# State updates of the samples as 32-row products from two row groups

## The chip, the cores and the metric

The kernel runs on the 8 cores of one Trainium2 chip. Each core takes one prompt of the batch of 8 and 16 of the 128 samples, and no core talks to another. The time is that of one execution on the device, in microseconds, of the slowest core. The median of three runs of the kernel before is 1225.57 us (1224.73 to 1225.89). Arrays are laid out and permuted on the host ahead of the launch and behind it; that is not part of the time.

## What is computed

Two layers, each with gated linear attention (4 heads, keys of 128, values of 256), a pooling branch and a merge of the two. The prompt has 16 meta tokens and 2048 tokens of its own. What matters here is the attention state of the samples. Each of a core's 16 samples brings 4 new tokens, and per layer and head a state S of 128 x 256 in float32. From the reference, for one sample and head, with b the cumulative log-forget over the 4 tokens:

```
o     = (intra-token part) + (q * exp(b)) @ S
kd    = k * exp(b_last - b)                       # 4 x 128
S_new = exp(b_last)[:, None] * S + kd.T @ v       # 128 x 256
```

All 16 x 4 x 2 = 128 states of a core are read, used for o, updated and written.

## The kernel before

*Tiling.* A core's tokens are 17 tiles: tile 0 holds the samples' 64 rows (sample s in rows 4s to 4s+3) and the 16 meta rows, 80 rows in all; 16 tiles of 128 prompt tokens follow. They are grouped in five chunks. Per layer and head, `att_unit` (L909) does the attention of a chunk: projections for k, q, v and the gate, scores, state recurrence, norm. For chunk 0 it also leaves the samples' operands: `kd0` (L473), the decayed keys of 80 rows by 128, `v0` (L471), the values of 80 rows by 256, and `q0`, the queries as 128 by 64.

*A batch of samples.* `sample_batch(l, h, j)` (L1064) updates the states of four samples of one head; j runs from 0 to 3, so there are 2 x 4 x 4 = 32 batches. Its work is emitted in three steps, parted by `yield`. First, GpSimd multiplies `kd0` with four columns of a row mask (`rowm`, a constant that is 1 in the four rows of one sample) into `kdm`: for each sample a copy of the 80 x 128 keys with all rows of other samples zero. A DMA on SyncE's queue brings the four states, ScalarE casts them to bf16, TensorE makes eight products of 4 columns for o, and VectorE copies these into `osT`. In the second and the third step, TensorE makes two products each, of all 80 rows of a masked key copy and of `v0`; both go to the two halves of one bank of PSUM, and VectorE then updates the two states in place by `scalar_tensor_tensor`. The third step ends with the DMA that writes the states. `sample_out` (L1097) later turns `osT` with float32 products into 64 partitions and adds it to the intra-token part.

*Banks.* Eight banks, in two groups of four that are handed out in turn (`bank`, L530): "P" for projections, "G" for all else, the sample products too.

*Order.* `weave` (L1149) alternates the steps of `att_unit` with those of `sample_batch` and others, which sets the order in which instructions are emitted. `list_schedule` (L145) then simulates the five engines with a cost for each instruction and fixes each engine's order: among the instructions that are ready, the one emitted first. A product's cost there is max(columns, 128) / 2.4 + 3 ns, whatever its rows. At run time each engine takes its instructions in that order and waits on semaphores.

*Helpers.* All products are issued at L551 and the transposes at L556, so the profile shows these lines; `tt` is L579, `stt` L591, `cp` L598 (L570 on ScalarE), `dma` L611. In the profile `kdm`, `osT` and the states are parts of `sb_Y`, `kd0` and `v0` of `sb_ar`, `q0` of `sb_zq`, `rowm` of `sb_invcnt`, and the decay factors are `sb_ebcm`.

Of the kernel before, what the change touches and what calls it, by code (L numbers as in the profile page):

```python
# [10 lines left out]
ALU = mybir.AluOpType  # L11
# [4 lines left out]
NCORE = 8  # L16
NSS = 16
TS = 4
NS = NSS * TS
NMETA = 16  # L20
NM = NS + NMETA
# [27 lines left out]
WP_C = WP_H + 4 * 6144  # L49
WP_O = WP_C + 8 * 3584  # L50
WP_TOT = WP_O + 8192

CF_IDENT = 0
CF_CAUS = 128
# [2 lines left out]
CF_ROWMASK = CF_INVCNT + 64  # L57
# [285 lines left out]
def make_consts():  # L343
    cf = np.zeros((128, NCF), np.float32)
    cf[:, CF_IDENT:CF_IDENT + 128] = np.eye(128, dtype=np.float32)
    j = np.arange(128)[:, None]
    i = np.arange(128)[None, :]
    cf[:, CF_CAUS:CF_CAUS + 128] = (j <= i).astype(np.float32)
    for a in range(NM):
        for b in range(NM):  # L350
            if a < NS and b < NS:
                ok = (a // TS == b // TS) and a <= b
            else:
                ok = a >= NS and b >= NS and a <= b
            cf[a, CF_MASKM + b] = 1.0 if ok else 0.0
    inv = np.zeros((4, NMETA), np.float32)
    for g, w in enumerate(WIN):
        for p in range(NMETA):
            inv[g, p] = 1.0 / min(w, p + 1)
    cf[:, CF_INVCNT:CF_INVCNT + 64] = inv.reshape(1, -1)  # L360
    for a in range(NM):
        cf[a, CF_ROWMASK + (a // TS if a < NS else NSS)] = 1.0
    for blk, m in ((0, 0), (1, 1), (2, 0), (3, 1), (4, 2), (6, 0)):
        cf[16 * blk:16 * blk + 16, CF_SPLIT + m] = 1.0
    return cf


def build_nc():
    nc = bass.Bass("TRN2", target_bir_lowering=False)

    def din(name, shape, dt=F32):
        return nc.dram_tensor(name, list(shape), dt, kind="ExternalInput").ap()

    def dout(name, shape, dt=F32):
        return nc.dram_tensor(name, list(shape), dt, kind="ExternalOutput").ap()
# [4 lines left out]
    sgla = din("sgla", [NL, NSS, 4, 128, 256])  # L380
    spool = din("spool", [NL, NSS, 15, 512])
    wpk = din("wpk", [NL, 128, WP_TOT])
    wal8 = din("wal8", [NL, 128, 512])
# [8 lines left out]
    nsg_s = dout("nsg_s", [NL, NSS, 4, 128, 256])  # L392
# [6 lines left out]
    with contextlib.ExitStack() as st:  # L399
# [48 lines left out]
        rowm = invcnt[:, 64:81]  # L448
# [18 lines left out]
        S_bfs, S_bfs_k = Y.take(1024, BF16)  # L467
        kdm, kdm_k = Y.take(2048, BF16)
        osT, osT_k = Y.take(128)
        ar1b = ar1[:, :].bitcast(BF16)  # L470
        v0, v0_k = ar1b[:, 0:256], ["v0"]  # L471
        on0, on0_k = ar1b[:, 256:512], ["on0"]
        kd0, kd0_k = ar1b[:, 512:640], ["kd0"]  # L473
# [3 lines left out]
        q0, q0_k = zq0[:, 2 * NM:2 * NM + NS // 2].bitcast(BF16), ["q0"]  # L477
# [33 lines left out]
        for i in range(2):  # L511
            a = X.take(512, at=2048 + i * 4096)
            b = X.take(512, at=2048 + i * 4096 + 2048)
            mrg.append((a, b))
        a = X.take(512, at=0)
# [14 lines left out]
        def bank(p):  # L530
            ids = pools[p]
            i = ids[bpos[p] % len(ids)]
            bpos[p] += 1
            S.bank_gen[i] = S.bank_gen.get(i, 0) + 1
            return banks[i], "B%d@%d" % (i, S.bank_gen[i])
# [4 lines left out]
        def fsz(ap):  # L540
            n_ = 1
            for d_ in list(ap.shape)[1:]:
                n_ *= int(d_)
            return n_

        def mm(out, lhsT, rhs, start, stop, r, w, sgc=False):
            N = fsz(rhs)
            c = max(N, 128 if N > 8 else 64) / 2.4 + 3.0
            if lhsT.dtype == F32:
                c *= 4.0  # L550
            return S.add("pe", lambda e: e.matmul(out, lhsT=lhsT, rhs=rhs, start=start, stop=stop,  # L551
                                                  skip_group_check=sgc), r=r, w=w, cost=c, lat=300.0, attach=True)
# [5 lines left out]
        def act(out, in_, func, r, w, bias=None, scale=None, accum_out=None):  # L558
            kw = {}
            if bias is not None:  # L560
                kw["bias"] = bias
            if scale is not None:
                kw["scale"] = scale
            if accum_out is not None:
                kw["accum_out"] = accum_out
            c = 180.0 + 0.83 * fsz(in_) + (210.0 if accum_out is not None else 0.0)
            if not isinstance(bias, (int, float, type(None))) or not isinstance(scale, (int, float, type(None))):
                c += 90.0
            tset = 1 if func == AF.Ln else (0 if func in (AF.Exp, AF.Tanh) else None)
            return S.add("act", lambda e: e.activation(out=out, in_=in_, func=func, **kw), r=r, w=w, cost=c, lat=150.0,  # L570
                         tset=tset)

        def ecost(eng, n_, f=1.0):
            if eng == "pool":
                return 250.0 + 1.7 * n_ * f
            return 130.0 + 1.06 * n_ * f

        def tt(eng, out, in0, in1, op, r, w, cost=None):
            return S.add(eng, lambda e: e.tensor_tensor(out=out, in0=in0, in1=in1, op=op), r=r, w=w,  # L579
                         cost=cost or ecost(eng, fsz(out)), lat=150.0)  # L580
# [9 lines left out]
        def stt(out, in0, scalar, in1, op0, op1, r, w):  # L590
            return S.add("dve", lambda e: e.scalar_tensor_tensor(out=out, in0=in0, scalar=scalar, in1=in1, op0=op0,  # L591
                                                                 op1=op1), r=r, w=w, cost=ecost("dve", fsz(out)),
                         lat=150.0)

        def cp(eng, out, in_, r, w):
            if eng == "act":
                return act(out, in_, AF.Copy, r, w)
            return S.add(eng, lambda e: e.tensor_copy(out=out, in_=in_), r=r, w=w,  # L598
                         cost=ecost(eng, fsz(out), 0.7 if eng == "dve" else 1.0), lat=150.0)
# [14 lines left out]
        def V(ap2d, nchunk, n):  # L614
            return ap2d[:, 0:nchunk * n].rearrange("p (c m) -> p c m", m=n)
# [448 lines left out]
        def sample_batch(l, h, j):  # L1064
            i = cnt["sin"] % 2
            cnt["sin"] += 1
            s_ap, sk = S_in[i]
            hp = h % 2
            em, emk = ebcm[:, 17 * hp:17 * hp + 17], "ebcm%d" % hp
            km = kdm[0:NM, 512 * j:512 * j + 512]  # L1070
            kmk = kdm_k[4 * j:4 * j + 4]
            tt("pool", V(km, 4, 128), kd0[0:NM, :].unsqueeze(1).to_broadcast([NM, 4, 128]),
               rowm[0:NM, 4 * j:4 * j + 4].unsqueeze(2).to_broadcast([NM, 4, 128]), ALU.mult, r=kd0_k + ["inv"], w=kmk)
            dma(V(s_ap, 4, 256), sgla[l, 4 * j:4 * j + 4, h].rearrange("s d v -> d s v"), r=[], w=sk)
            cp("act", S_bfs, s_ap, r=sk, w=S_bfs_k)
            bo, bok = bank("G")
            for sl in range(4):
                for d in range(2):
                    mm(bo[:, d * 16 + sl * 4:d * 16 + sl * 4 + 4], S_bfs[:, sl * 256 + d * 128:sl * 256 + (d + 1) * 128],
                       q0[:, (4 * j + sl) * 4:(4 * j + sl) * 4 + 4], True, True, r=S_bfs_k + q0_k, w=[bok])  # L1080
            cp("dve", V(osT, 2, 64)[:, :, 16 * j:16 * j + 16], V(bo, 2, 16), r=[bok], w=osT_k)
            for s2 in range(2):
                yield
                bp, bpk = bank("G")
                for jj in range(2):
                    s = 4 * j + 2 * s2 + jj
                    mm(bp[:, jj * 256:(jj + 1) * 256], kdm[0:NM, s * 128:(s + 1) * 128], v0[0:NM, :], True, True,
                       r=kmk + v0_k, w=[bpk])
                for jj in range(2):
                    s = 4 * j + 2 * s2 + jj  # L1090
                    o = (2 * s2 + jj) * 256
                    kx = sk[4 * (2 * s2 + jj):4 * (2 * s2 + jj) + 4]
                    stt(s_ap[:, o:o + 256], s_ap[:, o:o + 256], em[:, s:s + 1], bp[:, jj * 256:(jj + 1) * 256],
                        ALU.mult, ALU.add, r=kx + [emk, bpk], w=kx)
            dma(nsg_s[l, 4 * j:4 * j + 4, h].rearrange("s d v -> d s v"), V(s_ap, 4, 256), r=sk, w=[])

        def sample_out(l, h):  # L1097
# [97 lines left out]
        for l in range(NL):  # L1195
# [9 lines left out]
            def s_(*js):  # L1205
                return [(sample_batch(l, 0, j), 2.0) for j in js]
# [86 lines left out]
def _pack_weights(w_in, w_a, pool_w, w_b, w_out):  # L1293
    wp = np.zeros((NL, 128, WP_TOT), np.float32)

# [61 lines left out]
```

How the kernel before makes its waits and increments, by code:

```python
            def run_engine(ename, eng):  # L294
                seen = {}
                for op in ops:
                    if op["eng"] != ename:
                        continue
                    need = {}
                    for d in op["kept"]:
                        sk, val = ops[d]["token"]
                        if need.get(sk, 0) < val:
                            need[sk] = val
                    items = [(sk, val) for sk, val in need.items() if seen.get(sk, 0) < val]
                    attach = items.pop() if (items and op.get("attach")) else None
                    for sk, val in items:
                        eng.wait_ge(sems[sk], val)
                        seen[sk] = val
                    inst = op["fn"](eng)
                    if attach is not None:
                        inst._wait_ge(sems[attach[0]], attach[1])
                        seen[attach[0]] = attach[1]
                    if op["token"] is not None:
                        sk, val = op["token"]
                        inst.then_inc(sems[sk], 16 if op["dma"] else 1)
                if ename == "sp":
                    for k, v in self.dma_final.items():
                        sk = ("dma",) + k
                        if seen.get(sk, 0) < v:
                            eng.wait_ge(sems[sk], v)
```

## Time and profile before

| | before |
|---|---|
| median of three runs | 1225.57 us |
| the profiled execution | 1224.85 us |
| its span, slowest core (all: 1221.9 to 1223.1) | 1223.1 us |
| TensorE busy | 1151.9 us |
| VectorE / ScalarE / GpSimd busy | 676.9 / 573.5 / 467.0 us |
| granted TensorE clock, mean of the span | 0.988 |

One execution is profiled on every core; the rows are those of the slowest, core 1. The span is from its first to its last instruction. PE is TensorE's products, PEld its weight loads, DVE is VectorE, ACT ScalarE, POOL GpSimd, SP SyncE. Busy time is the union of the instructions' durations, and a product's duration reaches to its end, while the next one may start before that. A form such as 80\*128 80x256 is a weight of 80 rows and 128 columns and 80 rows of 256 columns that stream through it.

### The profile page before, as it was taken

The page shows a single profiled execution, that of the slowest core. Times are in us where ns is not written, and L with a number is a line of the kernel's source. Part 1 is how long each engine was busy: PE and PEld are TensorE (multiplying, and loading weights), DVE is VectorE, ACT ScalarE, POOL GpSimd, SP SyncE. Part 2 cuts the span into 40 slices and gives each one's busy share as a digit, 9 for nine tenths or more (in the row PEclk, how much of TensorE's full clock was granted, in tenths as well). Part 3 has the DMA queues.
Part 4 walks back from the last instruction along what each step waited for, and adds up shares of the span by engine and source line. Part 5 has one row for each costly group of instructions (what it writes and reads, how often), then busy time and mean ns, then how long its engine had stood idle before and what let it go on. Part 6 is the DMA issues. An engine that isn't in the chain of part 4 may idle for free.

```text
span 1223.1 us, 22742 instructions; the slowest of 8 cores (1221.9 to 1223.1 us)
## 1 busy us (share of the span) xinstructions
PE 1151.9 (94%) x7616; PEld 691.5 (57%) x7616; DVE 676.9 (55%) x1255; ACT 573.5 (47%) x1279; POOL 467.0 (38%) x754
## 2 busy tenths in 40 slices
PE   1579899999999999999999999999999999999997
PEld 1245457767676555555545555676777555555543
DVE  4466877766765222226776776666667422223555
ACT  2777665666564222222653744665665422222222
POOL 2467755333323222221136686344242222222221
PEclk9789999999999999999999999999999999999999
DMA  9461047362429123114465514725243923211544
GB/s 200 90 155 40 19 76 159 101 136 76 105 87 175 31 39 58 18 30 157 139 158 140 105 47 87 144 71 121 86 89 93 186 33 59 35 19 26 178 166 155
DMA packets 68591, 118.90 MB, mean 97 GB/s; under 512 B 4188, under 2 KB 46556, under 8 KB 68442
## 3 DMA queue, kind: packets, MB, share of 16 engines
q1 hardware_dynamic: 48570, 81.46, 20.9%
q0 software_dynamic: 19904, 35.98, 20.1%
q8 instruction: 60, 0.98, 0.3%
q14 instruction: 57, 0.47, 0.1%
HBM read 117.89 MB, written 36.24 MB: 126 GB/s over the span
## 4 chain that ended last, share of the span: by engine, by line
PE 85%; DVE 4%; ACT 3%; issue 3%; POOL 2%; DMA 1%; SPq 0%; DVEq 0%; POOLq 0%; ACTq 0%
PE bank L551 83%; PE bank L556 3%; DMA sb_OT<-wal 1%; POOL sb_OT L579 1%; ACT sb_Y L570 1%; DVE sb_X L598 1%; DVE sb_X L591 1%; ACT L570 1%; ACT sb_OT L570 1%; DVE sb_Y L585 0%; DVE sb_ast L579 0%; DVE sb_XN L579 0%; DVE sb_MB L811 0%; DVE sb_Y L591 0%; POOL sb_rst L579 0%
## 5 line engine op out<-in xcount | busy, mean ns | idle before, releaser
L551 PE MATMUL bank<-sb_XN,sb_RG 128*128 128x384 bf16 (+2 forms) x3280 | 664.4, 346 | 10.8 <-DVE sb_XN L579 4.4
L551 PEld LDWEIGHTS bank<-sb_XN,sb_RG 128*128 128x128 bf16 x3280 | 316.3, 98 | 248.1 <-issue 8.2
L591 DVE SCALAR_TENSOR_TENSOR sb_X<-sb_X,bank 128x384 f32<-128x384 f32 (+2 forms) x240 | 140.7, 594 | 255.1 <-PE bank L551 234.0
L570 ACT ACTIVATE sb_X<-bank,sb_halfc 128x384 f32<-128x384 f32 (+2 forms) x160 | 97.9, 615 | 250.0 <-PE bank L551 214.4
L570 ACT ACTIVATE sb_X<-bank 128x256 bf16<-128x256 f32 (+6 forms) x328 | 145.9, 464 | 96.2 <-PE bank L551 80.7
L579 POOL TENSOR_TENSOR sb_MB<-sb_X 128x384 bf16<-128x384 f32 (+2 forms) x80 | 88.0, 1100 | 203.7 <-DVE sb_X L591 203.3
L551 PE MATMUL bank<-sb_OT,sb_RG 128*128 128x384 bf16 (+2 forms) x680 | 143.6, 344 | 5.5 <-DVE sb_OT L591 4.2
L551 PE MATMUL bank<-sb_RG,sb_XN 128*128 128x256 bf16 (+1 forms) x1088 | 145.5, 272 | 1.1 <-ACT sb_OT L570 1.1
L570 ACT ACTIVATE sb_Y<-sb_Y 128x1024 bf16<-128x1024 f32 (+1 forms) x79 | 83.5, 1057 | 120.9 <-DVE sb_Y L591 101.6
L551 PE MATMUL bank<-sb_RG,sb_MB 128*128 128x512 bf16 (+1 forms) x544 | 125.3, 379 | 0.0
L579 POOL TENSOR_TENSOR sb_OT<-sb_OT 128x398 f32<-128x398 f32 (+12 forms) x122 | 112.5, 922 | 30.1 <-ACT sb_OT L570 14.0
L551 PEld LDWEIGHTS bank<-sb_RG,sb_XN 128*128 128x128 bf16 (+1 forms) x1088 | 104.5, 99 | 18.0 <-ACT sb_OT L570 1.4
L551 PEld LDWEIGHTS bank<-sb_OT,sb_RG 128*128 128x128 bf16 x680 | 66.5, 98 | 63.1 <-DVE sb_OT L591 7.3
L551 PE MATMUL bank<-sb_X 128*128 128x256 bf16 (+2 forms) x520 | 87.7, 259 | 2.4 <-DVE sb_X L598 2.2
L551 PEld LDWEIGHTS bank<-sb_RG,sb_MB 128*128 128x128 bf16 (+1 forms) x544 | 53.5, 99 | 57.9
L611 POOL DMA_DIRECT2D sb_RG<-wpk x60 | 45.9, 765 | 104.7 <-PE bank L551 74.2
L591 DVE SCALAR_TENSOR_TENSOR sb_OT<-bank,sb_halfc,sb_X 128x384 bf16<-128x384 bf16 (+1 forms) x80 | 47.8, 638 | 63.1 <-PE bank L556 63.1
L579 POOL TENSOR_TENSOR sb_X<-sb_X,sb_ebc 128x384 bf16<-128x384 bf16 (+1 forms) x40 | 35.1, 877 | 117.7 <-DVE sb_X L598 111.3
L551 PE MATMUL bank<-sb_YP,sb_RG 128*128 128x384 bf16 (+2 forms) x320 | 70.8, 343 | 0.0
L570 ACT ACTIVATE sb_OT<-bank 128x384 f32<-128x384 f32 (+6 forms) x120 | 48.3, 438 | 42.8 <-PE bank L551 28.2
L591 DVE SCALAR_TENSOR_TENSOR sb_X<-sb_X,sb_ebc,bank 128x256 f32<-128x256 f32 x128 | 60.5, 473 | 13.1 <-PE bank L551 12.9
L587 POOL TENSOR_SCALAR sb_rst<-sb_rst 128x1 f32<-128x1 f32 (+1 forms) x51 | 11.9, 233 | 139.9 <-ACT sb_Y L570 138.8
(94 smaller groups left out, 1202.8 us busy)
## 6 DMA issues: line engine op xcount, KB each, us to landing
sb_RG<-wpk POOLq DMA_DIRECT2D x40, 512.0 KB, 8.3
sb_Y<-sgla SPq DMA_DIRECT2D x32, 512.0 KB, 4.3
nsg_s<-sb_Y SPq DMA_DIRECT2D x32, 512.0 KB, 2.8
sb_Y<-xp SPq DMA_DIRECT2D x28, 512.0 KB, 5.1
sb_RG<-wpk POOLq DMA_DIRECT2D x16, 896.0 KB, 10.8
H<-sb_Y SPq DMA_DIRECT2D x16, 512.0 KB, 3.6
sb_Y<-H SPq DMA_DIRECT2D x16, 512.0 KB, 3.8
y_p<-sb_Y SPq DMA_DIRECT2D x16, 512.0 KB, 2.6
```

The lines of the kernel that those rows point to most:

```text
L551: return S.add("pe", lambda e: e.matmul(out, lhsT=lhsT, rhs=rhs, start=start, stop=stop, skip_group_check=sgc), r=r, w=w, cost=c, lat=300. ...
L556: return S.add("pe", lambda e: e.transpose(out, in_, ident), r=r, w=w, cost=c, lat=300.0, attach=True)
L570: return S.add("act", lambda e: e.activation(out=out, in_=in_, func=func, **kw), r=r, w=w, cost=c, lat=150.0, tset=tset)
L579: return S.add(eng, lambda e: e.tensor_tensor(out=out, in0=in0, in1=in1, op=op), r=r, w=w, cost=cost or ecost(eng, fsz(out)), lat=150.0)
L587: return S.add(eng, lambda e: e.tensor_scalar(out=out, in0=in0, scalar1=s1, scalar2=s2, op0=op0, op1=op1), r=r, w=w, cost=c, lat=150.0)
L591: return S.add("dve", lambda e: e.scalar_tensor_tensor(out=out, in0=in0, scalar=scalar, in1=in1, op0=op0, op1=op1), r=r, w=w, cost=ecost(" ...
L598: return S.add(eng, lambda e: e.tensor_copy(out=out, in_=in_), r=r, w=w, cost=ecost(eng, fsz(out), 0.7 if eng == "dve" else 1.0), lat=150.0)
L611: return S.add(eng, lambda e: e.dma_start(out=out, in_=in_, **kw), r=r, w=w, dma=True, after=after, cost=nb / 230.0)
```

## The change

The four products of a batch read 32 rows each in place of 80. Rows 0 to 31 hold samples 0 to 7 and rows 32 to 63 samples 8 to 15, so a batch now has two samples of the first half (2j, 2j+1) and two of the second (8+2j, 8+2j+1). `SPOS` gives a sample's place in the new order and `SINV` the sample at a place; the host permutes the states ahead and behind, the mask's columns are permuted in the constants, and the indices of queries and decay factors go through `SINV`. The mask product writes 64 rows instead of 80. The copy into `osT` becomes two copies of half the size. Both banks of a batch are taken in the second step, the four products are issued alternately from rows 0 to 31 (`a` = 0, first bank) and rows 32 to 63 (`a` = 1, second bank), and all four updates follow; the third step holds only the DMA that writes the states.

```diff
--- before.py
+++ after.py
@@ -49,6 +49,10 @@
 WP_C = WP_H + 4 * 6144
 WP_O = WP_C + 8 * 3584
 WP_TOT = WP_O + 8192
+
+
+SPOS = tuple(4 * ((s % 8) // 2) + 2 * (s // 8) + s % 2 for s in range(NSS))
+SINV = tuple(SPOS.index(i) for i in range(NSS))
 
 CF_IDENT = 0
 CF_CAUS = 128
@@ -359,7 +363,7 @@
             inv[g, p] = 1.0 / min(w, p + 1)
     cf[:, CF_INVCNT:CF_INVCNT + 64] = inv.reshape(1, -1)
     for a in range(NM):
-        cf[a, CF_ROWMASK + (a // TS if a < NS else NSS)] = 1.0
+        cf[a, CF_ROWMASK + (SPOS[a // TS] if a < NS else NSS)] = 1.0
     for blk, m in ((0, 0), (1, 1), (2, 0), (3, 1), (4, 2), (6, 0)):
         cf[16 * blk:16 * blk + 16, CF_SPLIT + m] = 1.0
     return cf
@@ -1067,31 +1071,36 @@
             s_ap, sk = S_in[i]
             hp = h % 2
             em, emk = ebcm[:, 17 * hp:17 * hp + 17], "ebcm%d" % hp
-            km = kdm[0:NM, 512 * j:512 * j + 512]
+            km = kdm[0:NS, 512 * j:512 * j + 512]
             kmk = kdm_k[4 * j:4 * j + 4]
-            tt("pool", V(km, 4, 128), kd0[0:NM, :].unsqueeze(1).to_broadcast([NM, 4, 128]),
-               rowm[0:NM, 4 * j:4 * j + 4].unsqueeze(2).to_broadcast([NM, 4, 128]), ALU.mult, r=kd0_k + ["inv"], w=kmk)
+            tt("pool", V(km, 4, 128), kd0[0:NS, :].unsqueeze(1).to_broadcast([NS, 4, 128]),
+               rowm[0:NS, 4 * j:4 * j + 4].unsqueeze(2).to_broadcast([NS, 4, 128]), ALU.mult, r=kd0_k + ["inv"], w=kmk)
             dma(V(s_ap, 4, 256), sgla[l, 4 * j:4 * j + 4, h].rearrange("s d v -> d s v"), r=[], w=sk)
             cp("act", S_bfs, s_ap, r=sk, w=S_bfs_k)
             bo, bok = bank("G")
             for sl in range(4):
+                s = SINV[4 * j + sl]
                 for d in range(2):
                     mm(bo[:, d * 16 + sl * 4:d * 16 + sl * 4 + 4], S_bfs[:, sl * 256 + d * 128:sl * 256 + (d + 1) * 128],
-                       q0[:, (4 * j + sl) * 4:(4 * j + sl) * 4 + 4], True, True, r=S_bfs_k + q0_k, w=[bok])
-            cp("dve", V(osT, 2, 64)[:, :, 16 * j:16 * j + 16], V(bo, 2, 16), r=[bok], w=osT_k)
-            for s2 in range(2):
-                yield
-                bp, bpk = bank("G")
+                       q0[:, s * 4:s * 4 + 4], True, True, r=S_bfs_k + q0_k, w=[bok])
+            for a in range(2):
+                cp("dve", V(osT, 2, 64)[:, :, 32 * a + 8 * j:32 * a + 8 * j + 8], V(bo, 2, 16)[:, :, 8 * a:8 * a + 8],
+                   r=[bok], w=osT_k)
+            yield
+            bps = [bank("G") for _ in range(2)]
+            for jj in range(2):
+                for a in range(2):
+                    p = 4 * j + 2 * a + jj
+                    mm(bps[a][0][:, jj * 256:(jj + 1) * 256], kdm[32 * a:32 * a + 32, p * 128:(p + 1) * 128],
+                       v0[32 * a:32 * a + 32, :], True, True, r=kmk + v0_k, w=[bps[a][1]])
+            for a in range(2):
                 for jj in range(2):
-                    s = 4 * j + 2 * s2 + jj
-                    mm(bp[:, jj * 256:(jj + 1) * 256], kdm[0:NM, s * 128:(s + 1) * 128], v0[0:NM, :], True, True,
-                       r=kmk + v0_k, w=[bpk])
-                for jj in range(2):
-                    s = 4 * j + 2 * s2 + jj
-                    o = (2 * s2 + jj) * 256
-                    kx = sk[4 * (2 * s2 + jj):4 * (2 * s2 + jj) + 4]
-                    stt(s_ap[:, o:o + 256], s_ap[:, o:o + 256], em[:, s:s + 1], bp[:, jj * 256:(jj + 1) * 256],
-                        ALU.mult, ALU.add, r=kx + [emk, bpk], w=kx)
+                    sl = 2 * a + jj
+                    s = SINV[4 * j + sl]
+                    kx = sk[4 * sl:4 * sl + 4]
+                    stt(s_ap[:, sl * 256:(sl + 1) * 256], s_ap[:, sl * 256:(sl + 1) * 256], em[:, s:s + 1],
+                        bps[a][0][:, jj * 256:(jj + 1) * 256], ALU.mult, ALU.add, r=kx + [emk, bps[a][1]], w=kx)
+            yield
             dma(nsg_s[l, 4 * j:4 * j + 4, h].rearrange("s d v -> d s v"), V(s_ap, 4, 256), r=sk, w=[])
 
         def sample_out(l, h):
@@ -1339,7 +1348,7 @@
             "xp": x_prompt[c],
             "xs": np.ascontiguousarray(x_sample[c * NSS:(c + 1) * NSS].reshape(NS, D)),
             "meta": meta_tokens,
-            "sgla": np.ascontiguousarray(state_gla[:, c * NSS:(c + 1) * NSS]),
+            "sgla": np.ascontiguousarray(state_gla[:, c * NSS:(c + 1) * NSS][:, list(SINV)]),
             "spool": np.ascontiguousarray(state_pool[:, c * NSS:(c + 1) * NSS]),
             "wpk": wpk, "wal8": wal8,
             "cols": cols, "fgfull": fgfull, "cf": cf,
@@ -1350,7 +1359,7 @@
     y_sample = np.concatenate([R[c]["y_s"].reshape(NSS, TS, D) for c in range(NCORE)], axis=0)
     nsg_p = np.stack([R[c]["nsg_p"] for c in range(NCORE)], axis=1)
     nsp_p = np.stack([R[c]["nsp_p"] for c in range(NCORE)], axis=1)
-    nsg_s = np.concatenate([R[c]["nsg_s"] for c in range(NCORE)], axis=1)
+    nsg_s = np.concatenate([R[c]["nsg_s"][:, list(SPOS)] for c in range(NCORE)], axis=1)
     nsp_s = np.concatenate([R[c]["nsp_s"] for c in range(NCORE)], axis=1)
     return (y_prompt.astype(np.float32), y_sample.astype(np.float32), nsg_p.astype(np.float32),
             nsp_p.astype(np.float32), nsg_s.astype(np.float32), nsp_s.astype(np.float32))
```

## Rows read from the trace of the kernel before

**Rows 1.** Busy time of the engines over the span, page: busy us (share), instructions.

```profile
PE 1151.9 (94%) x7616; PEld 691.5 (57%) x7616; DVE 676.9 (55%) x1255; ACT 573.5 (47%) x1279; POOL 467.0 (38%) x754
```

**Rows 2.** The chain that ended last, page: shares of the span by engine.

```profile
PE 85%; DVE 4%; ACT 3%; issue 3%; POOL 2%; DMA 1%; SPq 0%; DVEq 0%; POOLq 0%; ACTq 0%
```

**Rows 3.** Busy time by stretch, for three stretches with batches of samples.

```profile
core 1: us, PE busy (x) PEld busy (x) DVE busy (x) ACT busy (x) POOL busy (x), PEclk, DMA share, GB/s
...
230.00:300.00 70.00, 70.00 (x592) 50.81 (x591) 49.38 (x119) 44.63 (x122) 23.34 (x45) 1.00 0.43 107
300.00:500.00 200.00, 199.69 (x1334) 121.80 (x1332) 85.31 (x183) 80.46 (x193) 59.48 (x86) 1.00 0.38 78
780.00:960.00 180.00, 179.53 (x1472) 126.69 (x1470) 121.48 (x288) 109.51 (x309) 64.42 (x123) 1.00 0.45 105
```

**Rows 4.** TensorE's waits, 173 to 500 us: us in total, times, longest us.

```profile
PE bank L551 <- DVE sb_X L598: 1.0, 3, 0.4
```

**Rows 5.** Groups of instructions by line and shape: busy us, mean ns | idle before.

```profile
L591 DVE SCALAR_TENSOR_TENSOR sb_Y<-sb_Y,sb_ebcm,bank 128x256 f32<-128x256 f32 x128 | 55.2, 474 | 15.1 <-PE bank L551 14.7
...
L579 POOL TENSOR_TENSOR sb_Y<-sb_ar,sb_invcnt 80x512 bf16<-80x512 bf16 x32 | 33.7, 1064 | 0.0
...
L551 PE MATMUL bank<-sb_ar,sb_Y 80*128 80x256 bf16 x128 | 24.5, 273 | 0.0
...
L551 PE MATMUL bank<-sb_zq,sb_Y 128*128 128x4 bf16 x256 | 11.0, 165 | 0.0
L551 PEld LDWEIGHTS bank<-sb_ar,sb_Y 80*128 80x128 bf16 x128 | 11.0, 98 | 2.4 <-DVE sb_X L591 0.5 <-DVE sb_OT L591 0.4
...
L598 DVE COPY sb_Y<-bank 128x32 f32<-128x32 f32 x32 | 5.8, 183 | 0.2
...
L551 PE MATMUL bank<-sb_ident_f,sb_Y 128*64 128x128 f32 x32 | 5.2, 285 | 0.0
```

**Rows 6.** Order in time, TensorE, around products of batches: start us, us.

```profile
175.29 0.34 PE L551 MATMUL bank<-sb_zq,sb_Y 128*128 128x4 bf16 x8
...
181.17 0.60 PE L551 MATMUL bank<-sb_ar,sb_Y 80*128 80x256 bf16 x4
...
280.92 0.38 PE L551 MATMUL bank<-sb_ar,sb_Y 80*128 80x256 bf16 x2
281.14 1.04 PE L551 MATMUL bank<-sb_RG,sb_XN 128*128 128x256 bf16 x8
...
295.24 0.38 PE L551 MATMUL bank<-sb_ar,sb_Y 80*128 80x256 bf16 x2
295.46 0.49 PE L551 MATMUL bank<-sb_X 128*128 128x256 bf16 x3
```

**Rows 7.** Order in time, TensorE, around a transpose into 15 partitions.

```profile
159.91 1.03 PE L551 MATMUL bank<-sb_XN,sb_RG 128*128 128x512 bf16 x4
160.77 0.27 PE L556 MATMUL bank<-sb_ident_f,sb_OT 128*15 128x128 f32 x1
160.88 2.54 PE L551 MATMUL bank<-sb_XN,sb_RG 128*128 128x512 bf16 x13
```

**Rows 8.** Order in time, TensorE, around a float32 product into 64 partitions.

```profile
261.60 0.27 PE L551 MATMUL bank<-sb_ar 80*80 80x256 bf16 x1
261.80 0.65 PE L551 MATMUL bank<-sb_ident_f,sb_Y 128*64 128x128 f32 x4
262.38 0.82 PE L551 MATMUL bank<-sb_XN,sb_RG 128*128 128x512 bf16 x3
```

**Rows 9.** Order in time, TensorE's weight loads: eight loads in a row.

```profile
175.18 0.36 PEld L551 LDWEIGHTS bank<-sb_zq,sb_Y 128*128 128x128 bf16 x8
```

**Rows 10.** Order in time, VectorE, beside a batch: start us, us [idle before].

```profile
281.41 0.87 DVE L591 SCALAR_TENSOR_TENSOR sb_Y<-sb_Y,sb_ebcm,bank 128x256 f32<-128x256 f32 x2
285.23 1.14 DVE L591 SCALAR_TENSOR_TENSOR sb_OT<-bank,sb_halfc,sb_X 128x384 bf16<-128x384 bf16 x2 [2.94 <-PE bank L556]
286.29 0.86 DVE L591 SCALAR_TENSOR_TENSOR sb_Y<-sb_Y,sb_ebcm,bank 128x256 f32<-128x256 f32 x2
```

## The prediction

> **What bounds the kernel now.** I read the busy time of the engines first, then the chain of work that ended last, then the stretches in which the change lies, and last the waits of TensorE. TensorE is busy for 94% of the span [rows 1], and the chain that ended last runs through it for 85% [rows 2]. The 32 batches of samples lie between 173 and 390 us (layer 0) and between 760 and 955 us (layer 1). In the stretches there, TensorE is busy for 70.00 of 70 us, 199.69 of 200 and 179.53 of 180, at a granted clock of 1.00; VectorE is busy for 43 to 71% of them, GpSimd for about a third [rows 3]. From 173 to 500 us TensorE waits for another engine for 1.0 us in all [rows 4]. So the reader is to see an engine that runs from one product into the next: a microsecond of its work taken away is a microsecond of the span, and work added to an engine beside it costs nothing until TensorE has to wait for it.
>
> **What the changed products cost now.** They are the 128 products of 80 rows by 256 columns that write a bank from the decayed keys and values [rows 5]. The mean of 273 ns there is a latency and not a price, since the next product starts before the last one ends. Four in a row last 0.60 us, so one follows another after (0.60 − 0.273) / 3 = 109 ns [rows 6], although 48 of the 128 rows are unused. Most batches issue them as two pairs some 3 to 4 us apart: the pair at 280.92 us is followed by the next product at 281.14, the one at 295.24 by the next at 295.46 [rows 6]. That is 0.22 us a pair, 0.44 us a batch, and 32 × 0.44 = 14.1 us of TensorE's time. This is all that the change can touch, and half of it, 7.0 us, is the most that two row groups side by side can give.
>
> **The change, part by part.**
>
> The products. The same 128 are issued, each with 32 rows, in the order A0, B0, A1, B1, where A and B use disjoint rows of the array, weights of their own and banks of their own. A0 and A1 share rows and still need 109 ns each. No row shows two products in different row groups, so B0's delay behind A0 is bounded from both sides: 25 ns is the least distance between two products, that of the eight with 4 columns ((0.34 − 0.165) / 7 [rows 5, 6]), and 109 ns is no overlap at all. By form the nearest row is the 80-row product with its 109 ns, but it starts in the same rows as its neighbour; what keeps the products apart there is that both stream 256 columns through the same rows, and this reason is gone between A and B. I take 25 ns. The four then last 2 × 109 + 25 = 243 ns until the next product can start.
>
> Weight loads. There are still four of 128 columns a batch. Eight in a row, of 98 ns each, last 0.36 us, (0.36 − 0.098) / 7 = 37 ns apart [rows 5, 9], which fits twice beneath a product of 109 ns. That cover is thinner than today, because two loads now have to go beneath one product's time; if the load for A1 is not hidden, it adds at most its 98 ns [rows 5].
>
> Going from the whole array to 32 rows and back. Twice a batch, 64 times. One bound is nothing: the transpose into 15 partitions, which uses 15 columns of the array, starts at 160.77 us, just where the four products ahead of it let it (from 159.91 on, (1.03 − 0.38) / 3 = 0.217 each), and the next whole-array product starts 0.11 us behind it [rows 7], no later than float32 products follow one another in [rows 8] ((0.65 − 0.27) / 3 = 0.13). The other bound is the float32 product into 64 partitions: it starts 0.20 us behind a product that needs 0.11 (261.60 to 261.80 us), and the last of its four records, which ends at 262.45 and so starts at 262.18, is followed at 262.38 instead of 262.29 [rows 8]: some 95 ns on either side. That product differs in more than its columns, since it is sent as two passes (32 records of 16 products [rows 5]), so I take the transposes as the nearer row, and allow the 2 ns by which a pair of 80-row products exceeds 2 × 109 ns: two switches are 4 ns a batch.
>
> *Sum for TensorE:* 0.440 − (0.243 + 0.004) = 0.193 us a batch, 6.2 us over 32.
>
> The Trainium skill speaks against this: "TensorEngine Tiling (Array Packing)", Key Properties, says that a change of the tiling mode drains TensorE, while the tiles run independently. The rows of the 15-column transposes show no such drain for columns; no run here shows it for rows. With it the sum would be that of the third rival below. On the other side, "TensorE: Matmul & The Clock Gate", Part 3, gives 3.07 times for four row tiles of 512 columns, which no run here shows either; carried over to two tiles as 1.53 times, an estimate, a batch would take 0.436 / 1.53 = 0.285 us and 4.8 us would be saved.
>
> VectorE. The copy of the samples' outputs, 183 ns, is cut in two; each half is priced as the whole one, so 32 × 0.18 = 5.8 us are added beside other work. The four state updates of a batch (474 ns each [rows 5]) now come together, where two came first and two some 5 us later. At 281.41 us two take 0.87 us, and VectorE then idles for 2.94 us waiting for TensorE [rows 10]: the second pair (0.87) and the extra copy (0.18) fit in there, and the busy stretch from 286.29 us loses 0.87. I cost it at nothing. Without that cover it would be 32 × 1.05 = 34 us of delays on VectorE, of which only what TensorE waits for would count, and that is near nothing today.
>
> GpSimd, ScalarE, DMA. The mask product keeps its 512 elements (1064 ns) and loses 16 partitions, which I cost at nothing; the two transfers of a batch keep size and place in the order, since the store is still emitted at the third step. The permutation of samples is in the host's arrays, the constants and in the indices. The planner still gives each product 110 ns, so the order around the batches hardly changes; no other user of the second group of banks is emitted between the two places where a batch took its banks, so in the stretches with one batch per unit the banks fall to the same users as before. Cost: none, with ±1 us for shifted waits.
>
> **Against which time.** The profiled execution took 1224.85 us, its span 1223.1. Less 6.2 that is 1218.65; the median of the runs lies 0.72 us above the profiled execution, so 1225.57 − 6.2 = 1219.4 us.
>
> **The rivals.**
>
> *Side by side, but each switch costs what the float32 product pays.* For it: [rows 8]. Against it: [rows 7]. A batch takes 0.243 + 2 × 0.095 = 0.433 us, saves 0.007, in all 0.2: 1225.3 us, no change.
>
> *No overlap: the change doesn't do what it says.* For it: every row of the trace has products start a full column time apart, also those with unused rows. Against it: they all share rows. Four at 109 ns are 0.44 us a batch: 1225.6 us.
>
> *Slower: the array empties at every switch.* The place is the first product of 32 rows and the first whole one behind. The price is the rest of the latency of the product in flight, 273 − 109 = 164 ns, paid 64 times: 0.243 + 0.328 = 0.571 us a batch, 0.131 more than now, 4.2 in all: 1229.8 us. It decides from (0.440 − 0.243) / 2 = 98 ns a switch, beyond which the change loses. For it: the 95 ns of [rows 8], just short of that. Against it: [rows 7]. The rule of the Trainium skill cited above names this very mechanism.
>
> *The order around the batches gets worse*, say because four updates in a row make VectorE late for what TensorE needs next. The 2.94 us of idle time speak against it [rows 10]; if half of the 1.05 us reached TensorE in each batch, it would be 1225.57 − 6.2 + 17 = 1236 us.
>
> **How the numbers follow.** The forecast, overlap with cheap switches, gets 0.62; its own range is 1218.3 (the whole 7.0 us and some wait less) to 1223.5 us (B 60 ns behind A and 50 ns a switch, so 0.44 − 0.378 = 0.062 us a batch). The first rival gets 0.11, the second 0.11, the third 0.11, the fourth 0.05. The range goes from 1217.5 to 1226.5 us: it holds the forecast and the two rivals without change and leaves out the two slower ones and a little below. About 0.2% (2.45 us) is what a measurement can tell from no change here: faster by more 0.62, within it 0.22, slower by more 0.16.
>
> **What would show it.** Of the changed kernel's trace: the products appear as 128 of 32 rows; four in a row last about 0.273 + 0.134 = 0.41 us in place of 0.60, and what follows starts 0.25 us after the first. If the next product starts 0.44 us after it, the second rival holds if the four starts are 109 ns apart, the first if the starts are close and the gaps stand before and behind. At 0.57 the third does. TensorE's busy time should fall by about 6 us with its waits from 173 to 500 us still near 1 us; waits for VectorE there would be the fourth rival. The prediction is wrong if the span falls by less than 2 us, or by more than 7.3, for then something outside the batches moved.

## The result: slower by 1.1%

The changed kernel is slower. Its profiled execution took 1239.15 us, another 1239.04; against the kernel before the ratio is 1.011, with a 95% interval of 1.0094 to 1.0127. Two more executions took 1349.10 and 1354.68 us, with one die at a lower granted clock, and like all such executions they are left out here. The forecast was 1219.4 us and the range ended at 1226.5, so it was wrong in sign: 13.6 us were lost (1239.15 − 1225.57) where 6.2 were to be won. The span of the slowest core went from 1223.1 to 1237.0 us.

**The profile after.** The rows are those of core 1, here and in the experiments, unless another is named. The page's first part and chain, and the three stretches of [rows 3]:

```profile
PE 1165.4 (94%) x7616; PEld 684.5 (55%) x7616; DVE 681.3 (55%) x1287; ACT 573.9 (46%) x1279; POOL 467.1 (38%) x754
...
PE 86%; DVE 4%; ACT 3%; issue 3%; POOL 2%; DMA 1%; SPq 0%; DVEq 0%; POOLq 0%; ACTq 0%
```

```profile
230.00:300.00 70.00, 69.95 (x571) 47.60 (x570) 47.89 (x116) 43.91 (x123) 24.61 (x47) 1.00 0.38 99
300.00:500.00 200.00, 199.70 (x1328) 119.84 (x1328) 89.15 (x195) 81.81 (x194) 57.63 (x84) 1.00 0.39 81
780.00:960.00 180.00, 179.65 (x1447) 121.32 (x1446) 120.30 (x296) 107.91 (x302) 64.62 (x121) 1.00 0.39 98
```

TensorE is as full as in [rows 1, 3], at the same clock, but it does less in the same time: 571 products from 230 to 300 us where there were 592. Its busy time grew by 13.5 us, nearly as much as the span (13.9). So the loss is no wait of TensorE for another engine that the profile shows as idle time; it is in TensorE's own time, beneath the word "busy". TensorE's waits from 173 to 500 us, in all of the view (us in total, times, longest), are 1.7 us against 1.0 in [rows 4]:

```profile
PE bank L555 <- DVE sb_X L602: 0.9, 3, 0.4
PE bank L555 <- DVE sb_Y L595: 0.5, 1, 0.5
PE bank L555 <- DVE sb_X L595: 0.3, 1, 0.3
```

Where it goes is seen in the order of time of TensorE around one batch, beside [rows 6]:

```profile
285.85 0.49 PE L555 MATMUL bank<-sb_RG,sb_XN 128*128 128x256 bf16 x3
286.27 0.39 PE L555 MATMUL bank<-sb_ar,sb_Y 32*128 32x256 bf16 x2
286.59 0.28 PE L555 MATMUL bank<-sb_RG,sb_XN 128*128 128x256 bf16 x1
...
290.40 0.39 PE L560 MATMUL bank<-sb_ident_bf,sb_X 128*128 128x128 bf16 x4
290.72 0.39 PE L555 MATMUL bank<-sb_ar,sb_Y 32*128 32x256 bf16 x2
291.04 0.66 PE L555 MATMUL bank<-sb_XN,sb_RG 128*128 128x384 bf16 x3
```

Two things differ from what was forecast. First, there are still two pairs a batch, some 4 us apart, and not a run of four. Second, each pair has a gap on either side: three products of 109 ns from 285.85 on would let the pair start at 286.18, and it starts at 286.27; the pair needs 0.22 us and the next product starts 0.32 us behind its start. The two also don't overlap: they last 0.39 us, so they start 0.12 apart. The weight loads show where the gap arises, first those of the kernel before around the pair at 280.92 us [rows 6], then those of the place above:

```profile
280.81 0.21 PEld L551 LDWEIGHTS bank<-sb_ar,sb_Y 80*128 80x128 bf16 x2
281.04 0.64 PEld L551 LDWEIGHTS bank<-sb_RG,sb_XN 128*128 128x128 bf16 x6
```

```profile
286.27 0.11 PEld L555 LDWEIGHTS bank<-sb_ar,sb_Y 32*128 32x128 bf16 x2 [0.21 <-DVE sb_Y L602]
286.59 0.10 PEld L555 LDWEIGHTS bank<-sb_RG,sb_XN 128*128 128x128 bf16 x1 [0.21 <-issue]
286.60 0.26 PEld L560 LDWEIGHTS bank<-sb_ident_bf,sb_X 128*128 128x128 bf16 x3
```

In the kernel before, the pair's first load starts 0.11 us ahead of its product, beneath the product in flight, and so does the next load behind the pair. At a change between the whole array and a 32-row tile, the load starts only 0.20 us behind the start of the product in flight, at the moment at which its own product starts too: 286.27 for the first, 286.59 for the second. "issue" says that the profile shows no semaphore that held it; so it is in 61 of the 64 loads behind a run. On the way in the row above names a copy of VectorE's, which ended just then, but only 15 of the 64 first loads have such a name and the gap is the same in nearly all of them, so the copy is not its cause. The gap costs 286.27 − 286.18 = 0.09 us on the way in and 0.32 − 0.22 = 0.10 us on the way out. The Trainium skill, "TensorEngine Tiling (Array Packing)", Key Properties, says that a change of tiling mode drains TensorE. The trace agrees that a change costs time; the 0.20 us are less than the 0.27 that a product's record lasts, so the rows don't show a full latency paid. Read to the nanosecond over all runs, the median is 96 ns ahead of a run, and 200 ns instead of 109 from the start of its last product to the next: 91 ns.

The 32 batches have 64 such runs (61 are pairs), and 64 × 0.187 = 12.0 us of the 13.6. The other 1.6 us were not traced.

Why no alternation? The two products of a pair write the same bank: VectorE updates two states behind each pair, from one bank. The planner takes, of the ready instructions, the one emitted first. In the order that it fixes for this kernel, `bps[1]`, the bank of B, is free first in 29 of the 32 batches, and `bps[0]`, that of A, is still read by ScalarE, which scales the attention's outputs out of it. So B0 and B1 go first, and A0 and A1 some 4 us later. The trace has ScalarE's scaling between the two pairs:

```profile
287.98 1.21 ACT L574 ACTIVATE sb_X<-bank,sb_gst 128x256 bf16<-128x256 f32 x3 [0.24 <-POOL sb_gst L583]
```

The two products of a pair use the same rows, and in every pair they start 0.12 us apart.

### The profile page after: what moved, and what is told of

It is laid out like the page before. It is cut to its first block, busy times and chain, and to the rows that moved or that the text cites. A ratio compares the mean times of both kernels' runs of the same rounds, so it can differ in the third digit from the quotient of the medians.

```text
span 1237.0 us, 22760 instructions; the slowest of 8 cores (1234.4 to 1237.0 us)
## 1 busy us (share of the span) xinstructions
PE 1165.4 (94%) x7616; PEld 684.5 (55%) x7616; DVE 681.3 (55%) x1287; ACT 573.9 (46%) x1279; POOL 467.1 (38%) x754
## 4 chain that ended last, share of the span: by engine, by line
PE 86%; DVE 4%; ACT 3%; issue 3%; POOL 2%; DMA 1%; SPq 0%; DVEq 0%; POOLq 0%; ACTq 0%
PE bank L555 83%; PE bank L560 3%; DMA sb_Y<-xp 1%; POOL sb_OT L583 1%; ACT sb_Y L574 1%; DVE sb_X L602 1%; DVE sb_X L595 1%; DVE sb_MB L815 0%; ACT L574 0%; ACT sb_OT L574 0%; DVE sb_ast L583 0%; DVE sb_Y L595 0%; ACT sb_MB L574 0%; DVE sb_Y L589 0%; ACT sb_X L574 0%
```

## The experiments

Every kernel starts from the changed one unless said otherwise. Ratios are to the kernel before on the same chip.

**One run of four, alternating.** Each product claims both banks, so that all four wait for the later one.

```diff
-                       v0[32 * a:32 * a + 32, :], True, True, r=kmk + v0_k, w=[bps[a][1]])
+                       v0[32 * a:32 * a + 32, :], True, True, r=kmk + v0_k, w=[bps[0][1], bps[1][1]])
```

> The changed kernel with each of a batch's four products held until both banks are free, so that they are issued as one run A0, B0, A1, B1; nothing else is changed. In the changed kernel they went out as two runs, A0 A1 and B0 B1, each of one row group, with about 0.20 us more than the two products need around each run. Theory 1: what costs is the change between the whole array and a 32-row tile, about 95 ns on either side of a run, because the weight load behind the change starts only when the product in flight has left the array; 64 runs of 0.19 us are 12 us of the 13.6. Two questions then remain for this kernel: if the two row groups overlap, a batch takes 0.243 + 0.19 = 0.43 us and the time is about 1225.4 us; if they don't, it takes 0.436 + 0.19 = 0.63 us and the time is about 1231.7. Theory 2: each 32-row product is dearer by some 100 ns whatever stands around it: about 1239. Theory 3: the rest of the change (order, extra copies, later updates) costs the time: 1238 to 1240, as four products now wait for the later bank.

Measured: 1229.49 us, between the two cases, median of six (1228.90 to 1229.64). The interval of its ratio, 0.9948 to 1.0066, is too wide to use: of the ten executions of the kernel before that it is compared with, nine took 1223.56 to 1226.42 us and one 1240.38. The next kernel, with the same time, has a narrower one. Theory 2 falls, since 32-row products don't take 1239 us whatever stands around them. A batch, in TensorE's order of time and in its loads:

```profile
298.20 0.39 PE L560 MATMUL bank<-sb_ident_bf,sb_X 128*128 128x128 bf16 x4
298.52 0.39 PE L555 MATMUL bank<-sb_ar,sb_Y 32*128 32x256 bf16 x4
298.85 1.16 PE L555 MATMUL bank<-sb_RG,sb_XN 128*128 128x256 bf16 x9
```

```profile
298.52 0.11 PEld L555 LDWEIGHTS bank<-sb_ar,sb_Y 32*128 32x128 bf16 x4
298.84 0.88 PEld L555 LDWEIGHTS bank<-sb_RG,sb_XN 128*128 128x128 bf16 x9 [0.21 <-issue]
```

Four products last 0.39 us, as long as two before, and the next starts 0.33 us behind the first. The starts within a run are 3, 116 and 3 ns apart: the two row groups overlap almost wholly. The gaps on either side are unchanged. The sum over 32 batches: the overlap saves 32 × (0.438 − 0.232) = 6.6 us, the switches lose 32 × 0.187 = 6.0, so 0.6 us should be gained. Yet the kernel is 4 to 5 us slower than before; the hold for the later bank is left as the likely cause, and is tested below.

**The order A0, A1, B0, B1 in one run.** As the kernel above, with the two loops exchanged.

```diff
-            for jj in range(2):
-                for a in range(2):
+            for a in range(2):
+                for jj in range(2):
```

> As the run with alternation, one run of four 32-row products a batch once both banks are free, but in the order A0, A1, B0, B1, so that a change of row group comes once in a run and not three times. Theory 1: 32 runs instead of 64, so half of the loss goes: 0.436 + 0.19 = 0.63 us a batch, about 1231.7 us; if the two row groups overlap at the one place where they meet (A1 and B0), 0.35 + 0.19, about 1229. Compared with the alternating order, the difference is the overlap: 0 if there is none, up to 6 us if it is whole. Theory 2: 1239. Theory 3: as the alternating order.

Measured: 1229.07 us (1228.84 to 1229.79), ratio 1.004 (1.0025 to 1.0055). That is the 1229 given for half an overlap, but not for that reason: the alternating order takes the same time, and the run looks the same, with starts 7, 113 and 6 ns apart:

```profile
298.22 0.39 PE L560 MATMUL bank<-sb_ident_bf,sb_X 128*128 128x128 bf16 x4
298.54 0.39 PE L555 MATMUL bank<-sb_ar,sb_Y 32*128 32x256 bf16 x4
298.87 0.39 PE L555 MATMUL bank<-sb_RG,sb_XN 128*128 128x256 bf16 x2
```

**Which product starts second?** The order A0, A1, B0, B1 again, with B's products of 240 columns. The updates of B's states are narrowed in the same way, so their last 16 columns are left as they were.

```diff
+                    n_ = 256 - 16 * a
-                       v0[32 * a:32 * a + 32, :], True, True, ...
+                       v0[32 * a:32 * a + 32, 0:n_], True, True, ...
```

> The run with four 32-row products a batch issued A0, A1, B0, B1, but the products of the second row group (B) stream 240 columns, so that the trace tells them from A's; the last 16 columns of those samples' states are not updated. In the run with 256 columns for all, the starts were 0, 7, 120, 127 ns, the same pattern as in the alternating order. Theory 1: the two row groups have queues of their own behind the issue, so B0 starts beside A0 and ahead of A1: the order of the forms in time is 256, 240, 256, 240. Rival: products start in the order of issue, and the records' starts are not the real ones: 256, 256, 240, 240.

Measured in a single execution: 1230.21 us. The groups of TensorE's products in the 0.1 us from the start of a run, 287.50 to 287.60 us (the two transposes began ahead of it):

```profile
L555 PE MATMUL bank<-sb_ar,sb_Y 32*128 32x256 bf16 x1 | 0.3, 278 | 0.0
L560 PE MATMUL bank<-sb_ident_bf,sb_X 128*128 128x128 bf16 x2 | 0.3, 219 | 0.0
L555 PE MATMUL bank<-sb_ar,sb_Y 32*128 32x240 bf16 x1 | 0.3, 271 | 0.0
```

One product of A and one of B are under way before A1 has begun. So B0, issued third, starts second: 7 ns behind A0, in all 256 runs of the 8 cores. The third and the fourth start follow 113 ns later and within 2 ns of each other, A1 ahead of B1 in 86 runs and behind it in 170, so the expected order holds for the first two.

**80 rows again.** The mask product writes 80 rows again, too. The rest of the change stays: permutation, two copies, both banks in one step.

```diff
-                    mm(bps[a][0][:, jj * 256:(jj + 1) * 256], kdm[32 * a:32 * a + 32, p * 128:(p + 1) * 128],
-                       v0[32 * a:32 * a + 32, :], True, True, r=kmk + v0_k, w=[bps[a][1]])
+                    mm(bps[a][0][:, jj * 256:(jj + 1) * 256], kdm[0:NM, p * 128:(p + 1) * 128],
+                       v0[0:NM, :], True, True, r=kmk + v0_k, w=[bps[a][1]])
```

> The changed kernel with products of 80 rows of the masked keys again, so that no 32-row tile is used; the permutation, the two copies, both banks taken in one step and the order of issue stay as in the changed kernel. Theory 1 (the change of tile): the whole loss goes, 1225.5 us, within 1 us. Theory 2 (the 32-row product itself is dear): the same, 1225.5. Theory 3 (the rest of the change): 1237 to 1239 us, as the changed kernel.

Measured: 1226.03 us, ratio 1.001 (0.9998 to 1.0021). The gaps are gone:

```profile
286.12 0.39 PE L560 MATMUL bank<-sb_ident_bf,sb_X 128*128 128x128 bf16 x4
286.34 0.38 PE L555 MATMUL bank<-sb_ar,sb_Y 80*128 80x256 bf16 x2
286.56 1.95 PE L555 MATMUL bank<-sb_XN,sb_RG 128*128 128x384 bf16 x11
```

The rest of the change can't be told from nothing; its interval ends at 0.2%. Theory 3, that the rest of the change costs the loss, falls.

**64 rows.** Each product reads rows 0 to 63, of which only the sample's four are not zero.

```diff
-                    mm(bps[a][0][:, jj * 256:(jj + 1) * 256], kdm[32 * a:32 * a + 32, p * 128:(p + 1) * 128],
-                       v0[32 * a:32 * a + 32, :], True, True, r=kmk + v0_k, w=[bps[a][1]])
+                    mm(bps[a][0][:, jj * 256:(jj + 1) * 256], kdm[0:NS, p * 128:(p + 1) * 128],
+                       v0[0:NS, :], True, True, r=kmk + v0_k, w=[bps[a][1]])
```

> The changed kernel with each product reading all 64 sample rows, the 32 of the other half being zero in the masked keys. Theory 1: a product of 64 rows uses a tile smaller than the whole array too, so each run pays about 95 ns on either side: 64 x 0.19 = 12 us, 1237.5 to 1239 us. If only tiles of 32 rows pay it, 1225.5. Theory 2: depends on the rows, so 1225.5 to 1232. Theory 3: 1238 to 1239.

Measured: 1238.40 us (1238.26 to 1239.84), ratio 1.0116 (1.0093 to 1.0139): the whole loss, with the same gaps.

```profile
289.14 0.39 PE L560 MATMUL bank<-sb_ident_bf,sb_X 128*128 128x128 bf16 x4
289.46 0.39 PE L555 MATMUL bank<-sb_ar,sb_Y 64*128 64x256 bf16 x2
289.78 1.96 PE L555 MATMUL bank<-sb_XN,sb_RG 128*128 128x384 bf16 x11
```

16 rows fewer than 80 turn 0.22 us into 0.32. So the cause is neither the 32 rows nor the two row groups: products of 64 rows pay as much, and those of 80 nothing. Where between 64 and 80 it begins was not measured.

**80 rows, one run of four.** The hold without tiles: 80-row products, with keys and mask as in the 80-row kernel above, that claim both banks.

```diff
...
-                       v0[32 * a:32 * a + 32, :], True, True, r=kmk + v0_k, w=[bps[a][1]])
+                       v0[0:NM, :], True, True, r=kmk + v0_k, w=[bps[0][1], bps[1][1]])
```

> The run with alternation (one run of four products a batch, held until both banks are free), but with products of 80 rows, so that no tile changes and nothing overlaps. That run lost 3.9 us against the kernel before, although its products, overlap and switches together, cost 0.5 us less. Theory 1: holding all four products for the later bank and updating four states in a row makes TensorE wait elsewhere, some 4 to 5 us: this kernel then takes about 1229.5 to 1230.5 us. Rival: the 32-row runs disturb what follows them in some other way (weight loads, the order of the products behind), and the hold costs nothing: 1226.0 us, as the 80-row run without it.

Measured: 1229.99 us (1229.40 to 1230.19), ratio 1.0043 (1.0026 to 1.0059). So the hold costs about 4 us by itself, 1229.99 − 1226.03. With it 32-row products (1229.49) take half a microsecond less than 80-row ones, as the sum of overlap and switches would have it, but the two ranges overlap, so this difference is not shown. Part of what the hold does is seen in the waits of TensorE's weight loads from 160 to 960 us, first without it (80 rows, two pairs), then with it:

```profile
PEld bank L555 <- DVE sb_X L602: 6.4, 14, 0.9
```

```profile
PEld bank L555 <- DVE sb_X L602: 10.6, 23, 0.9
```

The casts of the running prompt state come 23 times too late instead of 14. Loads of transposes also wait for ScalarE, 3.3 us instead of 0.6. A wait of a load is not all lost time: TensorE itself stands idle for only 1.4 us more there (11.7 instead of 10.3). A likely reason for the later casts, argued and not separated from the later bank, is that four updates in a row stand ahead of them on VectorE.

**Ways around the hold.** Three kernels with alternating runs try to keep the overlap without it: the second bank from the projections' group; the bank of the batch's outputs as second bank; everything emitted one step later. For the second there is a control with 80 rows.

```diff
...
-            bps = [bank("G") for _ in range(2)]
+            bps = [bank("G"), bank("P")]          # first kernel
+            bps = [bank("G"), (bo, bok)]          # second kernel and its control
             yield
+            yield                                 # third kernel, ahead of the banks
```

> The run with alternation, but the second row group's bank is taken from the group of the projections, so that both banks are free early and the four products go out together at the time of the first pair. Theory 1: the waits of the hold go, overlap (-6.5 us) and 32 runs' switches (+6.0 us) remain: 1225 to 1226 us. If the hold is not what cost the 3.9 us, or the projections now wait for the borrowed bank: 1229 us or more.

> The run with alternation, but the second row group's products go into the bank that held the batch's outputs and that is free after the two copies; a batch takes two banks instead of three, and none of the projections'. The four go out together about 1 us after the output products, and no hold for a late bank is left. Theory 1: the hold's 4.5 us go, the products keep their 0.5 us of gain: 1225.0 us, between 1223.5 and 1227 us, since the order shifts. If the updates of four states in a row are what costs, and not the late bank: 1229.5 us.

> The same with products of 80 rows, no tile changes and no overlap: the control for the run before it in this list. Theory 1: 0.5 us slower than that one, 1225.5 us; if the banks saved help, both gain. If it is more than 2 us faster than that one, the runs of 32 rows cost something beside their overlap and their switches.

> The run with alternation, with both banks, products and updates emitted one step later. Theory: the late bank sets when the four go out, so the place in the order changes little but that the updates now rank behind the attention's own work on VectorE: if those waits are the 4.5 us, most of them go and the time is 1225 to 1227 us; if it is the bank alone, 1229.5 us.

Measured: 1237.33 us with a projection bank (ratio 1.0104, 1.0088 to 1.012), 1235.39 with the outputs' bank (1.0088, 1.0074 to 1.0102) and 1236.99 for its control (1.01, 1.0087 to 1.0114), 1229.08 one step later (1.0035, 1.0021 to 1.0049). All missed their hoped-for times, and none of them took the hold away. The second kernel's run was to follow about 1 us behind the output products; in its trace it does not:

```profile
281.89 0.35 PE L555 MATMUL bank<-sb_zq,sb_Y 128*128 128x4 bf16 x8
287.44 0.39 PE L555 MATMUL bank<-sb_ar,sb_Y 32*128 32x256 bf16 x4
```

Over all 256 runs the median from the start of the last output product to the run is 4.78 us with the hold (the first experiment), and 4.62, 4.82, 4.73 and 4.78 us in these four. Three of them replace B's bank and one moves the step; but the late bank is A's, `bps[0]`, and in the planner's order ScalarE's scaling still holds it in 28 or 29 of the 32 batches. So what the overlap is worth without the hold was not measured here. The last kernel's 1229.08 is what was foretold for the bank alone.

In the second, five of eight cores have spans of 1224.6 to 1227.0 us, but core 3, which sets the time, has 1233.6. Its ScalarE and TensorE waits from 880 us on (the first from 885):

```profile
ACT sb_Y L574 <- DMA sb_Y<-sgla: 8.0, 1, 8.0
```

```profile
PE bank L555 <- ACT sb_X L574: 6.4, 1, 6.4
```

A state arrives late on this core; its cast blocks ScalarE for 8.0 us, and TensorE stands idle for 6.4 us, to 905.1. Its granted clock is 0.50, the lower of its two levels (1.2 and 2.4 GHz), from 903 to 907 us, and 1.00 again from 909. On core 1 the same cast waits 0.5 us. The control shows the same on its slowest core (6.4 us for the state), so it is no matter of 32 rows; why the state is late was not found. In the first kernel TensorE waits 5.1 us, nine times, for VectorE's updates to free a bank, where it waits 0.5 us once in the changed kernel: in seven of the nine a projection waits, as its expectation allowed for the borrowed bank. The rest of its loss was not followed further.

**Runs of eight.** Two batches joined into one alternating run of eight products into four banks.

```diff
...
+            bps = [bank("G"), bank("G"), bank("P"), bank("P")]
+            allb = [b[1] for b in bps]
+            for jj in range(4):
+                for a in range(2):
+                    b = 2 * (jj // 2) + a
+                    p = 4 * (2 * jp + jj // 2) + 2 * a + jj % 2
+                    mm(bps[b][0][:, (jj % 2) * 256:(jj % 2 + 1) * 256], kdm[32 * a:32 * a + 32, p * 128:(p + 1) * 128],
+                       v0[32 * a:32 * a + 32, :], True, True, r=kdm_k + v0_k, w=allb)
...
```

The two batches' masks, loads and output products are now emitted ahead of the run, and the joined batches stand at half as many places between the attention units.

> Two batches joined: their eight products go out as one run, alternating between the two row groups, into two banks of either group; 16 runs in place of 32. Theory 1 by the run with alternation: overlap -6.5 us, switches 16 x 0.19 = 3.0 us, so 3.5 us less than before where the hold costs nothing: 1222 us; with waits for four banks at once and eight updates in a row of 3.8 us on VectorE it may lose 2 to 6 us of that: 1222 to 1228. If the switch were paid per product and not per run: 1226 or more even without waits.

Measured: 1247.14 us, ratio 1.0185 (1.0167 to 1.0204), far outside the 1222 to 1228 expected. The run itself does what it should: eight products, and the next starts 0.54 us behind the first, where 80-row pairs need 0.88.

```profile
299.86 0.61 PE L555 MATMUL bank<-sb_ar,sb_Y 32*128 32x256 bf16 x8
300.40 0.34 PE L560 MATMUL bank<-sb_ident_bf,sb_X 128*128 128x128 bf16 x3
```

The 0.54 us already contain the switch on the way out; with 0.10 us for the one on the way in, the runs gain 16 × (0.88 − 0.64) = 3.8 us. The rest of the kernel loses over 20. Of that, 8.6 us stand in 17 waits of TensorE's transposes for ScalarE from 160 to 960 us, a wait that the kernel before doesn't have there; the remainder was not followed further. The switch is paid per run and not per product, as theory 1 has it, but no kernel here turned longer runs into time. None beat the kernel before.

## Why the prediction was wrong

- *The bound.* Right: TensorE was and is the bound, and what its time lost went straight into the span (13.5 us of busy time, 13.9 of span). Layer 1's batches begin at 721 us and not at 760; nothing in the sum hangs on it.
- *The products' price.* Right: 0.22 us a pair, 14.1 us in all [rows 6].
- *Four in a row, A0, B0, A1, B1.* This step failed first. It took the order of emission for the order of issue. [rows 6] showed pairs 4 us apart; I read that as two steps of the generator, but one bank was held that long, and the planner goes by readiness. In the kernel before, the planner's order even has the third step's pair ahead of the second step's in 28 of the 32 batches. The prediction said that "the banks fall to the same users as before": they did, and at the same late time.
- *B's delay behind A, 25 ns.* The overlap exists, and is better than forecast, 3 ns, as soon as the run is one. In the changed kernel there was next to none: one of the 32 batches went out as a run of four, with starts at 0, 63, 120 and 182 ns.
- *The switch, 4 ns a batch.* This step failed in size, and it decides the sign. Both bounds were in the rows. I took the transposes as the nearer, because the float32 product differs in type and passes. But the trace before has float32 transposes into 64 partitions, of the same form as that product, and they show no gap:

```profile
642.22 0.81 PE L551 MATMUL bank<-sb_RG,sb_MB 128*128 128x512 bf16 x3
642.86 0.27 PE L556 MATMUL bank<-sb_ident_f,sb_OT 128*64 128x128 f32 x1
642.97 0.38 PE L551 MATMUL bank<-sb_RG,sb_MB 128*128 128x512 bf16 x1
```

So neither the type nor the 64 columns set the product of [rows 8] apart, and a product was the nearer row for products. Its 95 ns on either side are within a few ns of what was measured, 96 and 91. With two runs a batch it is paid 128 times instead of 64.

- *VectorE, GpSimd, the copies.* Right at nothing for the changed kernel: the 80-row kernel can't be told from the kernel before. The updates did not come in a row, as the pairs did not. Where they did, the hold cost 4 us, so nothing would have been too little for the run that was forecast.
- *The rivals.* Three had a part; the fourth, a worse order around the batches, had none in the changed kernel. "No overlap" held for the changed kernel, for another reason than the one given. The price of the first rival held, and the place and sign of the third: its 164 ns were too much, its 64 switches half of what there were. With no overlap and the upper bound together, one run a batch would have come out 32 × 0.19 = 6.1 us slower; the measured loss needs the second run a batch as well, 64 × 0.19 = 12 us. No case had these together, since the failing of the run and the price of the switch were taken one at a time.

## What to carry to other kernels

Before tiling the array by rows, count the runs, not the products: a run of small-row products between whole-array ones paid 0.19 us here, nearly what two products of 256 columns cost, so a run of four only breaks even. Check in the issued order that the products of different row groups can be ready together; a bank that comes free later splits the run and doubles the switches. Products of 80 rows were free of this, those of 64 were not, nor was the float32 product of 64 columns in [rows 8]. If a late bank splits the run, find out which one is late: here it was the first, and four kernels changed the other or the step.

## What the runs showed of the hardware that was not expected

- 64 rows pay the switch and 80 rows don't (0.32 against 0.22 us a pair), though both leave rows unused.
- Products of different row groups don't start in the order of issue: with A0, A1, B0, B1 the starts were A0, B0 (7 ns later), and 113 ns after that the other two. This was told apart in a single execution.
- Float32 transposes into 15 partitions [rows 7] and into 64 show no gap (the next product 0.11 us behind), while the float32 product into 64 partitions pays some 95 ns on either side [rows 8], as the change of rows does with 96 and 91. Products of 80 columns show none (109 ns to the next). Whether bfloat16 products of 64 columns or fewer pay is open.
